# Branch products of the gated merge as three products of split parts, with a ring of smaller units, in a hybrid diffusion step

## The reference, cut to what matters

```python
def merge_branches(y_pool, y_na, y_mla, g_logits, w_branch, w_out):
    ys = jnp.stack([y_pool, y_na, y_mla], axis=2)            # (B, T, 3, 512)
    proj = jnp.einsum('btnc,ncd->btnd', ys, w_branch)        # 512 -> 1024 for each branch
    gates = jax.nn.sigmoid(g_logits.reshape(B, T, 3, 1024))  # g_logits = h @ w_in[gate columns]
    return jnp.sum(gates * proj, axis=2) @ w_out
```

## Time and profile before

| | us |
|---|---|
| median of 3 runs | 2195.72 (2191.76 to 2199.2) |
| the profiled execution's own time | 2197.06 |
| its span, first to last instruction | 2194.9 |
| TensorE busy | 1945.7 (89%) |
| VectorE, ScalarE, GpSimd busy | 740.3, 527.7, 208.0 |
| mean granted clock of TensorE | 0.947 of full speed |

### The profile page before, as it was taken

How to read it: one execution, slowest core, us unless ns; L and a number is a source line. 1 busy time by engine, 2 the same in 40 slices (tenths; PEclk the granted TensorE clock), 3 DMA queues, 4 the chain that set the end, 5 groups by cost and what they waited for, 6 DMA issues and landing times.

```text
span 2194.9 us, 29069 instructions
## 1 busy us (share of the span) xinstructions
PE 1945.7 (89%) x11852; PEld 1508.4 (69%) x11852; DVE 740.3 (34%) x1374; ACT 527.7 (24%) x873; POOL 208.0 (9%) x208
## 2 busy tenths in 40 slices
PE   3799898989999997999918998989899999979992
PEld 1698555768888643888717975556688885548781
DVE  1422557642222135111163226466322122341113
ACT  1311261541111121111143104435311111201113
POOL 0202410010000000110041032100100000000104
PEclk8799999999999998999958999999999999989996
DMA  9413433121123308999782123121212223289995
GB/s 337 140 61 80 152 130 113 61 77 58 58 76 116 125 29 284 358 353 358 251 294 98 43 68 137 39 78 59 77 58 96 77 77 125 99 309 358 355 344 201
DMA packets 180776, 340.83 MB, mean 155 GB/s; under 512 B 9692, under 2 KB 88940, under 8 KB 180332
## 3 DMA queue, kind: packets, MB, share of 16 engines
q1 hardware_dynamic: 151164, 266.16, 34.6%
q10 hardware_dynamic: 21728, 44.83, 5.9%
q0 software_dynamic: 7776, 28.32, 3.6%
HBM read 309.50 MB, written 41.30 MB: 160 GB/s over the span
## 4 chain that ended last, share of the span: by engine, by line
PE 79%; DVE 10%; DMA 4%; issue 3%; ACT 2%; SPq 1%; POOL 1%; ACTq 0%; POOLq 0%; DVEq 0%
PE pair L1490 71%; PE opair L1490 5%; PE pair L1536 3%; DVE mid L1073 1%; DMA r<-mod_rows 1%; DVE r L1324 1%; ACT r L870 1%; SPq L468 1%; DMA ring<-in_w_mod 1%; DVE r_r L1159 1%; DVE mid L1085 1%; DMA ring<-in_w_up 0%; DMA ysT<-in_mod_aux 0%; DVE mid L965 0%; DVE mid L1197 0%
## 5 line engine op out<-in xcount | busy, mean ns | idle before, releaser
L1490 PE MATMUL pair<-r_r,mid_r 128*128 128x320 f32 (+2 forms) x2688 | 477.8, 314 | 0.0
L1490 PEld LDWEIGHTS pair<-r_r,mid_r 128*128 128x128 f32 x2688 | 416.8, 189 | 8.5 <-issue 1.2
L1490 PE MATMUL pair<-r,ring 128*128 128x128 f32 (+1 forms) x2432 | 323.6, 294 | 3.9 <-DMA ring<-in_w_up 2.6
L1490 PEld LDWEIGHTS pair<-r,ring 128*128 128x128 f32 x2432 | 299.5, 194 | 37.8 <-issue 18.3
L1490 PE MATMUL pair<-ring,hT 128*128 128x512 f32 (+1 forms) x640 | 231.0, 520 | 5.7 <-DVE hT L1175 3.5
L1536 PE MATMUL pair<-cst,mid 128*128 128x128 f32 (+1 forms) x668 | 108.5, 302 | 113.1 <-DVE mid L965 81.5
L1490 PEld LDWEIGHTS pair<-ring,hT 128*128 128x128 f32 x640 | 120.4, 190 | 108.5 <-issue 72.7
L1536 PEld LDWEIGHTS pair<-cst,mid 128*128 128x128 f32 (+1 forms) x668 | 83.0, 153 | 158.1 <-DVE mid L965 85.7
L1490 PE MATMUL pair<-ysT_r,mid_r 128*128 128x256 f32 (+1 forms) x768 | 171.5, 314 | 15.9 <-issue 15.9
L807 ACT ACTIVATE r<-pair 128x640 f32<-128x640 f32 x48 | 33.8, 704 | 463.3 <-PE pair L1490 463.3
L1490 PEld LDWEIGHTS pair<-ysT_r,mid_r 128*128 128x128 f32 x768 | 132.8, 195 | 16.7 <-issue 16.7
(11 more groups left out here) (231 smaller groups left out, 2136.0 us busy)
## 6 DMA issues: line engine op xcount, KB each, us to landing
ring<-in_w_mod SPq DMA_DIRECT2D x27, 2048.0 KB, 9.5
ring<-in_w_in SPq DMA_DIRECT2D x20, 2048.0 KB, 7.9
ring<-in_w_gate SPq DMA_DIRECT2D x34, 1024.0 KB, 6.9
ring<-in_w_up SPq DMA_DIRECT2D x34, 1024.0 KB, 11.9
ring<-in_w_down SPq DMA_DIRECT2D x34, 1024.0 KB, 10.7
expert_out<-r ACTq DMA_DIRECT2D x34, 512.0 KB, 7.5
ring<-in_w_branch SPq DMA_DIRECT2D x12, 1024.0 KB, 7.6
expert_out<-in_zeros SPq DMA_DIRECT2D x17, 512.0 KB, 12.8
```

Source lines behind the costliest of these rows:

```text
L1490: return nc.tensor.matmul(out, lhsT, rhs, start=first, stop=last, skip_group_check=True)
```

## The change

1. Branch products are split too. ScalarE rounds each group's branch weights (128 x 2048) and each branch's inputs (four blocks of 640 tokens) to float32r, and VectorE writes the remainders over the original, in place. A branch job is then 24 instructions instead of 16.
2. The gate halves' remainders are kept in place in the ring as well; only their high parts have a buffer of their own.
3. The ring is six units of 2048 columns. A gate half is a chunk of one unit, a branch chunk is one unit with a spare unit beside it for its high part. A gate half's unit is let go when its last gate job is filled, no longer when it is split.
4. The branches go in the order 1, 2, 0, and the pool jobs come after the fourth pair of the merge.
5. The copies and differences of the gate tokens go into the latent attention, one each in every third unit; GpSimd makes none.
6. `mergedT` lies elsewhere; `gb1` now shares its place with the pool branch's high inputs and `bc2` with the sigmoids, so that both are loaded after the last merge. `x2` is loaded as before.

The units by group of the merge, and what follows (`group_unit` gives (4 + 4g) mod 6): gate halves in u and u+1, branch in u+2, spare u+3; `("out", 0)` goes into units 4 and 5, `("out", 1)` into units 0 and 1, which the last group's two gate halves held.

```diff
-NSLOT = 3
-SLOT = 4096
+NUNIT = 6
+UNIT = 2048
-MERGE = [(m, n) for c in range(2) for n in range(3) for m in range(4 * c, 4 * c + 4)]
+BRANCHES = (1, 2, 0)
+GROUPS = [(c, n) for c in range(2) for n in BRANCHES]
+MERGE = [(m, n) for c, n in GROUPS for m in range(4 * c, 4 * c + 4)]
+LAST = MERGE[-1]
+POOL_AT = 3
...
+    for g, (c, n) in enumerate(GROUPS):
+        u = group_unit(g)
+        chunks += [(("gate", c, n, a), u + a, 1, ("gate", 4 * c + 2 * a + 1, n)) for a in range(2)]
+        chunks.append((("branch", c, n), (u + 2) % NUNIT, 1, ("branch", 4 * c + 3, n)))
+    u = group_unit(len(GROUPS))
+    chunks += [(("out", i), (u + 2 * i) % NUNIT, 2, ("y", TT - 1)) for i in range(2)]
...
     # ScalarE
+                def branch_high(g):
+                    key = ("branch", *GROUPS[g])
+                    await_landed(act, key)
+                    if g:
+                        c, n = GROUPS[g - 1]
+                        await_job(act, ("gate", 4 * c + 3, n))
+                    nc.scalar.copy(branch_parts(g)[0], ring_view(ring, key, NM, 512)).then_inc(b_high_ready, 1)
...
+                        if i % 3 == 1 and i // 3 < KD:
+                            k = i // 3
+                            nc.scalar.copy(g_high[k], h_t[:, k, :]).then_inc(g_high_ready, 1)
...
-                for k in range(KD):
-                    nc.scalar.copy(g_high[:, k, :], h_t[:, k, :]).then_inc(g_high_ready, 1)
+                act.wait_ge(pv_done, NU + len(ml_units) // 2)
                 split_high(N_WIN)
-                act.wait_ge(pv_done, NU + len(ml_units) // 2)
+                act.wait_ge(o_freed, NM)
+                branch_input_high(1)
+                branch_high(0)
                 split_high(N_WIN + 1)
...
+                    if i == 0:
+                        act.wait_ge(o_freed, 2 * NM)
+                        branch_input_high(2)
+                    if i % 4 == 2 and i // 4 + 1 < len(GROUPS):
+                        branch_high(i // 4 + 1)
...
+                await_job(act, ("gate", *LAST))
                 act.wait_ge(x_stored, L * (16 * TT) + 16)
                 act.dma_start(x2, x_res.rearrange("(t p) d -> p t d", p=P)).then_inc(x2_in, 16)
+                act.wait_ge(merged, KD)
+                await_mod_stored(act, 1)
+                for g in range(2):
+                    act.dma_start(gb1[:, g, :], mod_rows[g:g + 1, 2 * D:3 * D].partition_broadcast(P)).then_inc(gb_in, 16)
...
     # VectorE
+                        if i % 3 == 2 and i // 3 < KD:
+                            k = i // 3
+                            dve.wait_ge(g_high_ready, k + 1)
+                            V.tensor_tensor(g_low[:, k, :], h_t[:, k, :], g_high[k], ALU.subtract).then_inc(g_parts_ready, 1)
...
-                for k in range(0, KD, 2):
-                    dve.wait_ge(g_high_ready, k + 1)
-                    V.tensor_tensor(g_low[:, k, :], h_t[:, k, :], g_high[:, k, :], ALU.subtract).then_inc(g_parts_ready, 1)
                 split_low(N_WIN)
                 mod_rows_of(N_ML + 1)
                 await_mod_stored(dve, N_IN - 1)
-
+                branch_input_low(1)
+                branch_low(0)
                 split_low(N_WIN + 1)
...
     # TensorE
+                def branch_split(m, n, g):
+                    ps = pair_for(pe, ("branch", m, n))
+                    w = [x[:, :, m % 4 * P:(m % 4 + 1) * P] for x in branch_parts(g)]
+                    for a in (0, T // 2):
+                        for k in range(NM):
+                            last = three_products(ps[:, MID + a:MID + a + T // 2], [x[:, k, :] for x in w],
+                                                  [x[n][:, k, a:a + T // 2] for x in (y_high, y_low)], k == 0, k == NM - 1)
...
+                pe.wait_ge(g_parts_ready, KD)
+                for i, (m, n) in enumerate(MERGE):
+                    c, g = m // 4, i // 4
+                    channels_split(("gate", m, n), HALF_OF[(("gate", c, n, m % 4 // 2), m % 4 // 2)], m % 2 * P, by_channel)
+                    if i % 4 == 0:
+                        pe.wait_ge(b_parts_ready, g + 1)
+                        pe.wait_ge(y_parts_ready, (BRANCHES.index(n) + 1) * NM)
+                    branch_split(m, n, g)
+                    if i == POOL_AT:
+                        pool_products()
                 pe.wait_ge(merged, KD)
                 wa, wb = chunk(("out", 0), KD, 512), chunk(("out", 1), KD, 512)
```

More of the change, by code:

```diff
@@ L128, in plan_jobs @@
     jobs.append(("mod", N_ML + 1))
-    jobs += [("pool", g) for g in range(NM)]
-    for m, n in MERGE:
+    for i, (m, n) in enumerate(MERGE):
         jobs += [("gate", m, n), ("branch", m, n)]
+        if i == POOL_AT:
+            jobs += [("pool", g) for g in range(NM)]
     return jobs + TAIL
@@ new lines, in plan_ring @@
+def plan_ring(chunks):
+    unit_of, fill_of, released, fills, holder = {}, {}, {}, [0] * NUNIT, [None] * NUNIT
+    for key, u, n, release in chunks:
+        unit_of[key] = u
+        fills[u] += 1
+        fill_of[key] = fills[u]
+        released[key] = [h for i, h in enumerate(holder[u:u + n]) if h is not None and h not in holder[u:u + i]]
+        holder[u:u + n] = [(key, release)] * n
+        if key[0] == "branch":
+            holder[u + 1] = (key, release)
+    return unit_of, fill_of, released
@@ L223, in bass_hybrid_step @@
         w_low = [view(mid_r, (2 * i + 1) * PART, PART, k=KD) for i in range(2)]
+        gate_high = [view(mid_r, (2 + i) * PART, PART, k=KD) for i in range(2)]
         h_high, h_low = view(ysT_r, 0, TT * D, t=TT), view(r1_r, NQ_W, TT * D, t=TT)
-        g_high, g_low = view(r1_r, 0, KD * T, k=KD), view(r1_r, KD * T, KD * T, k=KD)
+        KEPT = 14336
+        g_high = [view(mid_r, k * T, T) if k < 6 else view(r1_r, KEPT + (k - 6) * T, T) for k in range(KD)]
+        g_low = view(hT_r, 0, KD * T, k=KD)
+        assert 6 * T <= 2 * PART and KEPT + 2 * T + MW <= R1_W
         xt = view(r1, KD * T, TT * D, t=TT)
@@ L538, in store_mods @@
                         stored[0] += 1
[L540 to L544, removed]
+                for key, _, _, _ in chunks:
+                    for before, release in RELEASED[key]:
+                        if release[0] == "parts":
+                            sp.wait_ge(parts_ready, release[1] + 1)
                         else:
-                            await_job(sp, last_reader)
+                            await_job(sp, release)
                         if before[0] == "mod":
@@ L1742, in _ @@
-                for m, n in MERGE:
-                    if m % 4 == 0:
-                        wb = chunk(("branch", m // 4, n), NM, 512)
-                    if n == 0 and m == 0:
-                        pe.wait_ge(g_parts_ready, KD)
-                    channels_split(("gate", m, n), HALF_OF[(("gate", m // 4, n), m % 4 // 2)], m % 2 * P, by_channel)
-                    if n == 0 and m == 0:
-                        await_read(pe, ("pool", NM - 1))
-                    if n == 2 and m == 0:
-                        pe.wait_ge(o_freed, 2 * NM)
-                    channels(("branch", m, n), wb, (m % 4) * P, NM, yT[n], T, MID)
+                def branch_split(m, n, g):
[5 more added lines that the diff above has]
+                                                  [x[n][:, k, a:a + T // 2] for x in (y_high, y_low)], k == 0, k == NM - 1)
+                    last.then_inc(filled[PAIR_OF[("branch", m, n)]], 1)
@@ new lines, in pool_products @@
+                def pool_products():
+                    pe.wait_ge(small_in, 80)
+                    pe.wait_ge(pooled, NM)
+                    for g in range(NM):
+                        ps = pair_for(pe, ("pool", g))
+                        wg = wpool_sb[:, g * P:(g + 1) * P]
+                        mm(ps[:, 1024 - T:512], wg, u_pad[:, g, C_AT:C_AT + N_CTX], True, True)
+                        mm(ps[:, 512:1024], wg, u_pad[:, g, L_AT:L_AT + N_LAT], True, True)\
+                            .then_inc(filled[PAIR_OF[("pool", g)]], 1)
```

159 lines of the change are left out of this document (96 added, 63 removed).

## The result

| | before | after |
|---|---|---|
| median of 4 runs | 2195.63 us | 2181.45 us (2179.95 to 2181.47) |
| ratio to before | | 0.9936, 95% interval 0.9925 to 0.9948 |
| profiled execution's own time | 2197.06 | 2181.45 |
| its span | 2194.9 | 2179.6 |
| TensorE busy | 1945.7 | 1911.7 |

The account below looks back on a forecast made before the run. TensorE, busy 89% of the span, was taken as the bound. Terms of -18.7 -10.35 +1.4 +4.3 +11.9 +2.0 = -9.45 us a layer, -18.9 for two, took the profiled 2197.06 to 2178; range 2170 to 2188.

Parts of the forecast that it names:

- Branch jobs: Merge: 24 split instructions take 3.52 us instead of 4.30, so 24 jobs save 18.7 us a layer.
- the count of passes: Alternative price for branch products: three of four passes save 1.07 us a job, 25.8 us a layer; not used.
- The beginning: Start of the merge: first gate job 10.35 us earlier, then a new 1.4 us stall before the first branch job.
- Pool jobs: Moved into the merge, the four pool jobs lie on the path and cost 4.3 us a layer.
- Insertions into the latent attention: Gate-token copies and differences fit holes of ScalarE and VectorE: 0 us, or 11.1 if nothing were hidden.
- Splits in the merge: Branch weight and input splits are hidden at later groups; a sigmoid comes 1.9 us late; uncovered cost 3.5.
- The end: Before the first y job: output weights land 17 us after issue beside x2, adding 11.9 us a layer.
- The clock: After a gap of 12 us the y jobs start at half clock for 4 us: +2.0 us a layer.
- A: Rival at the merge's end: output weights land after 8.5 to 12 us; total 2157 to 2168; chance 0.28.
- B: Rival in the latent attention: each insertion costs a unit's turn, 2.43 us; total 2217; chance 0.05.
- C: Rival in the merge: 24 split branch instructions cost 4.30 us like 16 plain ones; total 2215; chance 0.03.
- D: Rival: half-exposed latent attention insertions (11 us) and 0.7 at five merge groups (7); 2196 with both; chance 0.14.

Follow-up runs that it names:

- e4: Kernel after with plain float32 branch products and without the splits of branch weights and inputs; 2212.08 us.
- e7: e3 with the four pool jobs moved between the first gate job and the first branch job; 2146.85 us.
- e5: Kernel after with the gate tokens' eight copies and eight differences moved back behind the latent attention; 2189.05 us.
- e6: Kernel after with the eight gate-token insertions in eight latent attention units in a row instead of every third; 2178.93 us.
- e1: Kernel after with the load of x2 held until the second half of the output weights has landed; 2156.85 us.
- e3: Kernel after with the output weights' second half loaded as two chunks, each awaited only where used, and x2 loaded after them; 2145.34 us.

## Why the prediction was right, and where its terms were off

- *Branch jobs*, 0.78 each: 3.52 measured, exact; shown alone by e4. The weighing against the count of passes was right too: with four passes for true float32 (the Trainium skill, "FP8 and Floating Point Precision", section "TensorE Precision Notes") the sum would have been 7 us a layer too good. This case's trace doesn't agree that three passes cost three quarters: they cost 3.52 of 4.30, 0.82.
- *The beginning*: 4.43 after the modulation job's start, 4.4 forecast. The first branch job started 12.82 after it (468.74 - 455.92), as forecast (470.1 less 457.28), so the new wait is 1.35 for 1.4.
- *Pool jobs*: 4.3 forecast. They show 4.49 in e7's timeline, with a modelled end. Between the pair ahead of them and the pair behind them the kernel after leaves 4.31 us (the multiplication at 504.92 less the 0.68 by which it is late, and the sigmoid at 515.59 less the 7.04 of its gate job). e7 showed that they stay on the path, but could have covered the wait at the first group.
- *Insertions into the latent attention*: 0 forecast, 0.14 shown (e5, e6).
- *Splits in the merge*: the cover was right. The sigmoid of a group's last gate job comes 1.86 us late (8.90 after the multiplication before it instead of 7.04), and the multiplication behind it 0.68 late, where 1.9 and 0.7 were forecast, and TensorE loses nothing by it: it waits for branch parts once in each layer, at the first group. In the timeline of the kernel after, 672 to 690 us:

```profile
674.05 1.90 ACT L725 CAST ring_r<-ring 128x2048 fp32r<-128x2048 f32 x1 [9.91 <-PE pair L1596]
675.85 0.70 ACT L881 ACTIVATE r<-pair 128x640 f32<-128x640 f32 x1
...
678.19 0.82 DVE L1276 TENSOR_TENSOR r<-pair,r 128x640 f32<-128x640 f32 x1
...
684.55 0.70 ACT L881 ACTIVATE r<-pair 128x640 f32<-128x640 f32 x1 [6.20 <-PE pair L1596]
```

- *The end*: the mechanism was right, the landing was 18.6 instead of 17. The step that mis-sized it took the loaded landing of the earlier trace rows as nearly sufficient; there the weights were issued 4.4 us behind the other transfer, which was that much nearer its end. The gap between the last branch job and the first y job was 15.7 (735.26 less 719.57, the multiplication's start less 0.18), against 13.8 forecast. TensorE's wait of 15.55 is also beyond the 8 to 13 that the prediction gave as the sign of being right, a range that its own 13.8 didn't fit.
- *The clock*: 2.0 forecast, 2.8 shown (30.50 against 27.73). The step took 4 us at half speed from the earlier trace rows; here it was 6.
- *The sum.* It was -18.9, measured -14.2 between the medians; by the stretches of the table and the y jobs it is (-9.94 + 2.77) + (-10.21 + 2.84) = -14.5. So the sum was too good by 4.4. The end's two terms are off by 1.9 and 0.8 a layer, 5.4 for both. About 1 came back, mostly from two things that the prediction left out. The first gate job of each layer took 7.64 us from its start to its sigmoid in the kernel before and takes 7.31 in the kernel after. And the gap in front of it was not 14.77 but 15.02 in the second layer (1557.22 - 1542.20), where the granted clock was 0.50 from 1554 to 1556, under the pool jobs.
- *The closeness of 2178 to 2181.45* flatters the sum. It was added to the profiled execution, which stands 1.4 above the median of the kernel before; from the median the same sum gives 2176.7. And the forecast's own range of 2170 to 2188 is wider than the landings of 14 to 19 that it names: by the same sum these give 2172 to 2182, and the real landing uses nearly all of that.

Of the rivals, A was refuted by the wait for the output weights; e1 shows what it would have needed, the engines for the weights alone. B fell by e5 and e6, C by e4. Of D's two losses, the insertions cost 0.14 us a layer instead of 5.5, and the splits at later groups nothing.

In the profiled pair the layers look uneven: from the first window product of one layer to that of the next the first layer is 8.7 us shorter, and from there to the end the second is 4.8 shorter. The stretch of the change is alike in both. Two other pieces differ. From the first y job to the first expert round it is 144.36 and 141.61 us in the kernel before, and 144.73 and 144.79 in the kernel after. So the slow clock, which costs 3.2 in the second layer, shows as only 0.4 in the first, where the kernel before takes 2.75 longer than in its second layer; its chain has a wait of 11.85 us for the modulation weights there, at 846.43, which the second layer's chain doesn't have. That this wait is the reason wasn't tried. And ahead of the stretch, from the first window product to the modulation job, it is 378.90 and 376.81 us before, 379.34 and 379.52 after, 374.73 and 376.95 in e3, whose code is the same there as in the kernel after. What sets that scatter wasn't tried either.

## What to carry to other kernels

When a buffer is let go at a later event than before, look for the last chunk in the chain: all others may have slack, and the last one's landing time then stands in front of whatever comes next. Price it under the load that starts with it, not alone: here the same 2 MB took 8.0 us alone and 18.6 beside a transfer with rows twice as long, and moving that other transfer, which nobody needed yet, was worth more (21.5 us by the stretch and the y jobs) than the change itself (14.5). Work for engines with holes in their schedule can go into a stage where TensorE is busy all the time, as long as it is smaller than the holes; sixteen operations cost 0.14 us there.

## What the runs showed of the hardware that was not expected

- **A gap of 4.9 us costs as much clock as one of 15.5.** In e1 TensorE waited 4.9 us and its first two y jobs took 30.41 us, in the kernel after 15.5 and 30.50. With the 1.78 us of e3 they take 27.73, but this is not a safe length: in the second layer of e7 they took 29.43 after the same 1.78, at a granted clock of 0.61 and 0.54 in their first 4 us. What set that one apart wasn't tried. In e5 a gap of 5.36 us put the gate products at 0.50 too.
- **Half speed lasted for about 6 us of work**, in the y jobs of the kernel after (735 to 741) and in the split gate products of e5 (462.4 to 468), where the split products at 78 us had it for 4. So it is not the kind of product that tells them apart; what does wasn't tried.
- **Eight insertions in a row were as free as spread ones**, though in each period of 4.87 us they fill 1.4 of ScalarE's hole of 1.55 us and 1.6 of VectorE's 1.75.
